# Written-out program, vectors in dense stretches, FFN norm sums about a shift: one step of a hybrid decoder

## The reference

```
x <- LN(alpha*x + 1/2*(1+g1)*SwiGLU_1(mod(x; s1, sc1)))
x <- LN(alpha*x + (1+g2)*W_out[pool_mix(u_A) | gelu(u_G)*RGLRU(conv(u_B))]),  [u_A|u_B|u_G] = mod(x; s2, sc2) @ W_in
x <- LN(alpha*x + 1/2*(1+g3)*SwiGLU_2(mod(x; s3, sc3)))
mod(x) = x*(1+scale(c)) + shift(c);  the nine vectors s1, sc1, g1, ... g3 of a layer come from silu(c) @ W_ada + b_ada
LN: mean, variance, (x-mean)*rstd, times ln_g, plus ln_b
SwiGLU: (silu(h @ w_gate) * (h @ w_up)) @ w_down, 21 tiles of 128 wide
```

## Time and profile before

| what | value |
|---|---|
| time, median of 3 runs | 1088.82 us (1086.84 to 1091.44) |
| span of the profiled execution, its own time | 1091.2 us |
| PE busy | 1016.7 us, 93% of the span |
| DVE busy | 647.9 us, 59% |
| ACT busy | 552.8 us, 51% |
| POOL busy | 104.8 us, 10% |
| moved by transfers | 234.46 MB, 215 GB/s on the mean |

### The profile page before, as it was taken

How to read it: one execution, slowest core, us unless ns; L and a number is a source line. 1 busy time by engine, 2 the same in 40 slices (tenths; PEclk the granted TensorE clock), 3 DMA queues, 4 the chain that set the end, 5 groups by cost and what they waited for, 6 DMA issues and landing times. The chain is left out here.

```text
span 1091.2 us, 25203 instructions
## 1 busy us (share of the span) xinstructions
PE 1016.7 (93%) x9660; PEld 983.8 (90%) x9660; DVE 647.9 (59%) x909; ACT 552.8 (51%) x642; POOL 104.8 (10%) x195
## 2 busy tenths in 40 slices
PE   5799999998997999999969999999799889999996
PEld 3699999987995999999959999999698779999995
DVE  1455554558797754556465545454869885555554
ACT  1556564244664656553237565533539456565432
POOL 8000000005001700000040000000310050000000
PEclk9699999999999999999989999999899999999998
DMA  9898856796679576655678976498747956655621
GB/s 290 264 280 231 227 166 234 232 317 226 224 260 319 142 213 164 187 168 186 204 236 230 258 222 188 152 319 284 255 145 275 315 160 190 188 161 172 194 76 40
DMA packets 279223, 234.46 MB, mean 215 GB/s; under 512 B 7328, under 2 KB 240922, under 8 KB 279123
## 3 DMA queue, kind: packets, MB, share of 16 engines
q1 hardware_dynamic: 277040, 229.70, 68.0%
q0 software_dynamic: 1792, 2.54, 0.9%
q10 hardware_dynamic: 306, 1.12, 0.3%
HBM read 232.06 MB, written 1.78 MB: 214 GB/s over the span
## 5 line engine op out<-in xcount | busy, mean ns | idle before, releaser
L853 DVE TENSOR_TENSOR w_lo<-raw,w_hi 128x2048 fp32r<-128x2048 f32 x156 | 358.3, 2298 | 255.9 <-ACT w_hi L688 255.3
L439 PE MATMUL bank<-m_hi,w_hi 128*128 128x264 f32 x1664 | 479.9, 288 | 18.8 <-DVE m_lo L897 14.8
L440 PE MATMUL bank<-m_lo,w_hi 128*128 128x264 f32 x1664 | 476.6, 286 | 0.0
L441 PE MATMUL bank<-m_hi,w_lo 128*128 128x264 f32 x1664 | 476.0, 286 | 0.0
L688 ACT ACTIVATE w_hi<-raw 128x2048 fp32r<-128x2048 f32 x156 | 298.2, 1911 | 170.3 <-PE bank L441 122.0
L439 PEld LDWEIGHTS bank<-m_hi,w_hi 128*128 128x128 f32 x1664 | 318.3, 191 | 22.0 <-DVE m_lo L897 16.2
L440 PEld LDWEIGHTS bank<-m_lo,w_hi 128*128 128x128 f32 x1664 | 318.4, 191 | 0.1
L441 PEld LDWEIGHTS bank<-m_hi,w_lo 128*128 128x128 f32 x1664 | 316.9, 190 | 0.0
L439 PE MATMUL bank<-h_hi,w_hi 128*128 128x264 f32 x672 | 192.2, 286 | 0.0
L441 PE MATMUL bank<-h_hi,w_lo 128*128 128x264 f32 x672 | 191.1, 284 | 0.0
L440 PE MATMUL bank<-h_lo,w_hi 128*128 128x264 f32 x672 | 191.0, 284 | 0.0
(11 more groups left out here) (180 smaller groups left out, 649.6 us busy)
## 6 DMA issues: line engine op xcount, KB each, us to landing
raw<-in_ffn_wgu_dram SPq DMA_DIRECT2D x168, 512.0 KB, 5.1
ada_raw<-in_w_ada_dram SPq DMA_DIRECT2D x72, 1024.0 KB, 8.9
raw<-in_ffn_wdown_dram SPq DMA_DIRECT2D x48, 512.0 KB, 3.6
raw<-in_ffn_wdown_dram SPq DMA_DIRECT2D x48, 384.0 KB, 4.2
raw<-in_w_in_dram SPq DMA_DIRECT2D x24, 512.0 KB, 10.5
raw<-in_w_out_dram SPq DMA_DIRECT2D x16, 384.0 KB, 3.9
raw<-in_w_out_dram SPq DMA_DIRECT2D x8, 256.0 KB, 3.2
x_rows<-in_x_prompt_dram ACTq DMA_DIRECT2D x1, 1024.0 KB
```

The lines of the kernel that those rows point to most:

```text
L439: pe.matmul(out, hi, r_hi, start=start, stop=False)
L440: pe.matmul(out, hi, r_lo, start=False, stop=False)
L441: mm = pe.matmul(out, lo, r_hi, start=False, stop=stop)
L853: dve.tensor_tensor(w_lo[:, slot], raw[:, slot], w_hi[:, slot].bitcast(F32), ALU.subtract)\
```

## The change

The program is written out: no loop over layers and none over UP units, so each of the 18 vectors and each unit has its own place (a vector's number is 9 times the layer plus its index from s1 = 0 to g3 = 8).

- A table `AFTER` gives the place of each vector on PE: (8, 1) puts the first half of vector 2 behind unit 8, its second half behind unit 9, the transposes behind the next. Nine vectors stand in UP and DOWN stretches (2, 3, 4, 8, 9, 10, 12, 13, 14), three in the gap of an FFN norm (5, 11, 15), 6 and 16 in the mixer, 7 behind unit 43 inside OUT of layer 0, 17 behind the variance of the mixer norm of layer 1, 0 and 1 at the start. `LOAD_BEHIND` puts its load into SP's queue.
- The FFN norm's sums are taken about a shift, the mean of the first four tiles, which DVE subtracts from all eight before the last two are finished. Sums of z and of its square over tiles 0 to 5 go to PE before the last product, and what follows is a mean and a square matmul for each of the tiles 6 and 7. DVE makes the variance as the mean of squares less the square of the mean.
- Normalising is one operation per tile on DVE, z times coefficient times rstd (`full`), ACT adds the shift and rounds to m_hi, and one more on DVE makes m_lo (`low`); the mean is subtracted in pairs of tiles between them.
- The first two units behind a norm are taken together, tile by tile: 12 matmuls for each tile of m_hi and m_lo.
- POOL's `finish_x` begins when the third unit behind the norm is split.
- Units of DOWN and OUT are split over their own width. In OUT the second half goes over tiles 0 and 1, then 2 to 4, then 5 to 7, residuals are added one tile at a time, and the split of the first unit of the next FFN stands between the residuals of tiles 1 and 2.

```diff
+    AFTER = {2: (8, 1), 3: (15, 1), 4: (24, 1), 5: (32, 0), 6: (38, 0), 7: (43, 0), 8: (54, 1), 9: (62, 1),
+             10: (71, 1), 11: (77, 0), 12: (89, 1), 13: (96, 1), 14: (104, 1), 15: (110, 0), 16: (116, 0),
+             17: (122, 0)}
...
+    LOAD_BEHIND = {2: (4, 5)}
+    for a in range(3, VECTORS):
+        first, apart = AFTER[a - 1]
+        LOAD_BEHIND[a] = (first + 6, first + 6 + apart)
...
-                def norm_beside(i, v, after):
-                    ada_part(v, 0)
-                    mean(i)
-                    ada_rest(v)
-                    variance(i)
-                    ada_part(after, 0)
-                    if i == 1:
-                        turn_rows()
-                    ada_part(after, 1)
+            def beside(g):
+                if g in FIRST_HALF:
+                    ada_part(FIRST_HALF[g], 0)
+                if g - 1 in FIRST_HALF:
+                    ada_part(FIRST_HALF[g - 1], 1)
+                if g - 2 in FIRST_HALF:
+                    ada_turns(FIRST_HALF[g - 2])
...
+            def up_phase(l, f, together, vector):
+                g0 = l * UNITS + UP[f]
+                for j in range(together):
+                    ready(pe, g0 + j)
+                for k in range(DT):
+                    pe.wait_ge(m_ready, l * MODS + f * (DT + 2 + DT) + k + 1)
+                    for j in range(together):
+                        product(bank[2 * j][:, 0:T], *weight((g0 + j) % SLOTS, k), m_hi[:, k], m_lo[:, k],
+                                k == 0, k == DT - 1, gate_done)
+                        product(bank[2 * j + 1][:, 0:T], *weight((g0 + j) % SLOTS, DT + k), m_hi[:, k], m_lo[:, k],
+                                k == 0, k == DT - 1, units_done)
...
+                            if pair == 3 and third == 2 and i == 1:
+                                pe.wait_ge(sums_ready, 2 * l + f + 1)
+                                stat(bank[MEAN], mean_w, zsum[:], True, False)
+                                stat(bank[VAR], mean_w, sqs[:, 0], True, False)
...
+                        if pair == 2 and third == 0:
+                            pe.wait_ge(first_sum, 2 * l + f + 1)
+                            stat(bank[MEAN], shift_w, zsum[:], True, True).then_inc(shift_out, 1)
+                        beside(g)
...
+            def ffn_stats(l, f):
+                n, s = l * 3 + 2 * f, l * 14 + f * 9
+                pe.wait_ge(evicted, n * DT + 7)
+                stat(bank[MEAN], mean_w, z[:, 6], False, False)
+                pe.wait_ge(squared, s + 4)
+                stat(bank[VAR], mean_w, sqs[:, 6], False, False)
+                pe.wait_ge(evicted, n * DT + 8)
+                stat(bank[MEAN], mean_w, z[:, 7], False, True).then_inc(mean_out, 1)
+                pe.wait_ge(squared, s + 5)
+                stat(bank[VAR], mean_w, sqs[:, 7], False, True).then_inc(var_out, 1)
...
+                act.wait_ge(rows_out, l + 1)
+                if l:
+                    act.wait_ge(rows_stored, l * 6 * 16)
+                act.activation(s_rows[0:96], bank[ROWS][0:96, :], ACT.Copy).then_inc(rows_ready, 1)
+                if l:
+                    ada_copies(17)
+                act.wait_ge(var_out, l * 3 + 2)
...
-                    own.did(dve.reciprocal(rstd[:], rstd[:]))
-                    own.wait()
-                    for m in range(DT):
-                        o = dve.tensor_tensor(z[:, m, 0:TP], z[:, m, 0:TP], rstd[:, 0:TP], ALU.mult)
+                def full(m):
+                    dve.scalar_tensor_tensor(sq[:, m, 0:TP], z[:, m, 0:TP], coef[:, 0, m, 0:1], rstd[:, 0:TP],
+                                             ALU.mult, ALU.mult).then_inc(scaled, 1)
+                def low(m):
+                    dve.wait_ge(m_hi_done, first + (m + 2 if m else 1))
+                    return dve.scalar_tensor_tensor(m_lo[:, m, 0:TP], sq[:, m, 0:TP], coef[:, 1, m, 0:1],
+                                                    m_hi[:, m, 0:TP].bitcast(F32), ALU.add, ALU.subtract)
...
+                full(1)
+                for m in range(2, DT):
+                    if m in late:
+                        subtract_mean(m)
+                        dve.wait_ge(less_mean, n * DT + m + 2)
+                    full(m)
+                    low(m - 1).then_inc(m_ready, 1)
+                low(DT - 1).then_inc(m_ready, 1)
...
+                    if i == 7:
+                        dve.wait_ge(shift_out, k + 1)
+                        shift = wide(bank[MEAN][:, 0:T], 2)
+                        for a in (0, 2):
+                            dve.tensor_tensor(z[:, a:a + 2], z[:, a:a + 2], shift, ALU.subtract).then_inc(centred, 1)
+                        for a in (4, 6):
+                            own.did(dve.tensor_tensor(z[:, a:a + 2], x[:, a:a + 2], shift, ALU.subtract))
...
+                split(g0 + 4)
+                split(g0 + 5)
+                tiles_done = l * 7 + 1
+                dve.wait_ge(tile_done, tiles_done + 1)
+                residual([(0, 0)], G2, x, evicted)
+                dve.wait_ge(units_done, g0 + 4)
+                residual([(1, 1)], G2, x, evicted)
+                n = l * 3 + 1
+                dve.wait_ge(evicted, n * DT + 2)
+                own.did(dve.tensor_tensor(zsum[:], z[:, 0], z[:, 1], ALU.add))
+                split(g0 + 6)
+                for m in (2, 3, 4, 5, 6, 7):
+                    if m in (4, 7):
+                        dve.wait_ge(units_done, g0 + (5 if m == 4 else 6))
+                    else:
+                        tiles_done += 1
+                        dve.wait_ge(tile_done, tiles_done + 1)
+                    residual([(m, m)], G2, x, evicted)
...
+            def finish_x(l, i):
+                n = l * 3 + i
+                pool.wait_ge(rstd_ready, n + 1)
+                ready(pool, l * UNITS + (IN, UP[1], UNITS)[i] + 2)
+                for m in range(DT):
+                    pool.wait_ge(less_mean, n * DT + m + 1)
+                    pool.tensor_tensor(x[:, m], z[:, m], rstd[:], ALU.mult).then_inc(x_scaled, 1)
+                    pool.wait_ge(x_scaled, n * DT + m + 1)
+                    pool.tensor_scalar(x[:, m], x[:, m], ln_g_of(l, i)[:, m:m + 1], ln_b_of(l, i)[:, m:m + 1],
```

More of the change, by code:

```diff
@@ new lines, in _, with product, weight @@
+            pe.wait_ge(init_read, 1 + DT)
+            def product(out, hi, lo, r_hi, r_lo, start, stop, done=None):
+                pe.matmul(out, hi, r_hi, start=start, stop=False)
+                pe.matmul(out, hi, r_lo, start=False, stop=False)
+                mm = pe.matmul(out, lo, r_hi, start=False, stop=stop)
+                if stop and done is not None:
+                    mm.then_inc(done, 1)
+                return mm
+            def weight(slot, i):
+                return w_hi[:, slot, i * P:(i + 1) * P], w_lo[:, slot, i * P:(i + 1) * P]
@@ L674, in _ @@
+                t.then_inc(fin_out, 1)
         @block.scalar
@@ new lines, in mixer @@
+                if l == 0:
+                    ada_copies(vector + 2)
+                act.activation(spare[:], eps[:], ACT.Sqrt)
+                for a in range(0, DT, 2):
+                    square(sq[:, a:a + 2], z[:, a:a + 2], less_mean, (l * 3 + 1) * DT + a + 2)
+                act.wait_ge(rows_out, l + 1)
[4 more added lines that the diff above has]
+                    ada_copies(17)
@@ new lines, in mixer @@
+                dve.wait_ge(mean_out, n + 1)
+                dve.wait_ge(evicted, (n + 1) * DT)
+                for a in range(0, DT, 2):
+                    dve.tensor_tensor(z[:, a:a + 2], z[:, a:a + 2], wide(bank[MEAN][:, 0:T], 2), ALU.subtract)\
+                       .then_inc(less_mean, 2)
+                if l == 0:
+                    finish_vector(vector + 2)
+                coefficients(l, 2)
+                split(g0 + 7)
+                dve.wait_ge(less_mean, (n + 1) * DT)
+            split(0)
```

1330 lines of the change are left out of this document (728 added, 602 removed).

## The result

The changed kernel took 1072.14 us (median of 4 runs, 1071.33 to 1072.58), the kernel before 1088.26 (4 runs, 1086.84 to 1091.44) on the same chip: ratio 0.986, 95% interval 0.983 to 0.988. On a second chip, beside 13 runs of the kernel before, it was 1072.24 against 1091.58, ratio 0.983 (0.981 to 0.986). So it is faster, by 16 to 19 us, where the forecast of 1056 promised 33. The direction and the range held; the size did not.

A forecast was written before the change was run, and what follows sets the result against it. Dense stretches were taken as bound by PE's own work, with norms and the end between them. Terms summed to −32.5 from a span of 1091.2, giving 1058.7 and, with 2.4 off, 1056 us; range 1036 to 1080.

The forecast's parts named there:

- The FFN norm of 7.1: Last to first product around an FFN norm falls from 19.9 to about 7.1 us; two such norms give −25.6.
- the end of 16.4: The end, without subtract, squares and eight variance matmuls in series, falls from 21.6 to about 16.4 us: −5.2.
- the clock of the first units: First units behind three norms start at clock 1.00 after shorter PE idle, 1.7 us less each: −5.1.
- the price of a dense vector: A vector in dense FFN stretches costs 4.1 us; nine stand there instead of four: +20.5.
- the second FFN of layer 0: Layer 0's FFN 2 and its norm, the stage's terms together: −10.5 us.
- rival B: Partial stalls in dense stretches from GpSimd's x operations meeting DVE, up to 32 us: 1068–1088, at worst 1089; chance 0.15.
- rival C: Vector loads in lumps of 2–4 MB ahead of raw loads starve dense code: 1150 if nothing is absorbed; chance 0.07.
- the mixer norm: DVE's split waits for a raw behind 4 MB of vector; layer 0 gains 0.8, layer 1 loses 2.3: +1.5.
- Moves in the start, waits for splits of pairs and the parameter preparation cancel: These three effects were costed at nothing, taken to cancel within 1.4 us.
- The base: The sum used the profiled span of 1091.2; the shown runs' median, 1088.82, is 2.4 lower, taken off at the end.
- A: The raw is there in time and the mixer norms shrink too: −21, 1035 us; chance 0.20.

The follow-up runs named there:

- e7: The changed kernel without the wait that keeps GpSimd's pass over x behind the third unit's split: 1088.16 us.
- e2: The changed kernel with vector 17's halves read behind the last FFN's first and second units instead of ahead of the first: 1060.09 us.
- e3: The changed kernel with loads of vectors 7 and 17 reading only 64 of 2048 columns of each chunk: 1049.32 us.
- e6: The changed kernel with vector 7 read earlier, vector 17 moved into UP, vector 7's copies ahead of splits, DVE's split between residuals 4 and 5: 1045.70 us.
- e9: The changed kernel with PE multiplying the identity by itself behind OUT in the mixers, 7 and 52 products: 1069.17 us.
- e12: e6 with GpSimd's transfers of layer 1's parameter and state rows and state copies behind the split of unit 1: 1042.92 us.
- e10: e6 with the transfer of x_prompt issued by SP ahead of the first vector chunk instead of by ACT beside it: 1045.66 us.
- e1: The changed kernel with DVE's split of the next FFN's first unit moved behind the mixer norm's subtraction: 1063.72 us.
- e4: The kernel before, unchanged, profiled a second time: span 1091.5 us, time 1093.07 us.
- e5: The changed kernel, unchanged, run again on another chip with a second profile: 1072.24 us.
- e11: The changed kernel with the nine UP and DOWN vectors computed by 32 matmuls instead of 128, the rest left out: 1070.85 us.

## Why the prediction was right, and where it was wrong

**Right, and at the forecast size.** The FFN norm of 7.1 (measured 7.1 three times), the end of 16.4 (16.9), the clock of the first units (forecast −5.1; the first 96 products behind the three norms take 12.3 instead of 13.6, 14.3 and 14.2, together −5.2), the price of a dense vector (4.3 for 4.1), and with it the second FFN of layer 0 (−10.5 forecast, −11.7 measured). The norm's terms up to the reciprocal add up to 4.9, where the prediction writes 5.2; the trace has 5.1, because DVE's subtract for tiles 0 and 1 ends behind the root. For the end's 16.4 no terms are shown. The pass of GpSimd, rival B, leaves no gap above 0.40 us on PE where the change put it; e7 shows that it costs 16 us beside the norm. Lumps of vector loads in dense code, rival C, were absorbed: behind the start PE has no gap above 0.40 in the UP and DOWN stretches.

**The step that failed in size: the mixer norm.** The mechanism was named (the split between the residuals, behind 4 MB), and e2, e3 and e6 show it. The term was priced at +1.5, and the two stages came out 7.9 above their forecast (11.3 by the second profiles). Two parts show in the rows. The raw came 19.9 and 19.6 us behind the issue of the first chunk (311.72 to 331.60, 821.31 to 840.94), where 18.1 was worked out from the earlier trace rows: 1.5 to 1.8 each, and no run shows why. And the chain behind the last residual was priced at full clock: it took 12.8 in layer 0 instead of 10.4, and 16.3 in layer 1 instead of 13.5. Of that e9 gives back 2.0 and 1.5 by keeping PE busy ahead of it. The row of the kernel before that said 0.71 for a statistics matmul stood in a stretch with clock 1.00. In the changed kernel PE had waited 13.2 ahead of these matmuls in layer 1, and 2.7 and 3.2 in layer 0 with only two transposes in between; the clock was 0.54 and 0.50, and such a matmul took 0.9 to 1.25. SP's issue, 0.7 later in the stage than forecast, adds to it, and the residuals took about half a microsecond less. The stage that all this was compared with was a long one, too: in the second profile of the kernel before the two norms take 21.8 and 22.7, where the earlier trace rows has 24.3.

**The step that failed by being left out: the start.** "Moves in the start, waits for splits of pairs and the parameter preparation cancel" was taken without looking at what GpSimd's queue carries there. The start and the first FFN came out 5.0 above forecast, 4.7 of it in three parts. The first product is 1.6 later: e12 shows the rows of layer 1 behind this, and e10 shows that the order of x is not. PE's transposes of layer 1's parameters now stand among layer 0's products, 1.3 from 67.66, where before they stood in the norm between the layers (563.52):

```profile
67.66 0.57 PE L433 MATMUL bank<-ident,st_rows 120*128 120x120 f32 x4
...
68.78 0.25 PE L433 MATMUL bank<-ident,q_rows 36*128 36x36 f32 x1
```

And the first 96 products took 1.8 longer, 1.5 of it in the second unit at clock 0.77. That part is not the change's: the second profile of the kernel before has it too, and e1 does not. What decides it is not shown.

**The base.** Four more microseconds lie between the profiled span, a long execution's, and the median off which the difference was taken (e4, e5). A difference of spans, −20.6, was compared with a difference of medians, −16.1 on one chip and −19.3 on the other.

**What the rivals were worth.** A, the mixer norms shrinking too, needed the raw in time: it is e6, 1045.7, with all the work. A's own 1035 had layer 1's norm at 13.2 (344.1 behind 330.9), short even of the 13.5 (344 to 357.5) that the prediction gives the chain with vector 17 in it; with the raw in time and vector 17 in its place that norm took 18.9 (e3). The prediction did not ask what other order SP's queue could have; the order chosen cost 23 us (e3), more than the whole change gained.

## What to carry to other kernels

A transfer that nobody needs yet, written ahead of one that an in-order engine waits for, can cost its whole landing time (here 4 MB, 11.5 us in e2). Look at what each engine has queued behind the wait: moving one instruction (e1) handed the wait to the next engine, while moving the transfer (e2, e6) removed it. When a loop is written out, loads that were once a layer's own start may all fall into the first microseconds, where everything waits for transfers (e12). Price PE's work behind a long wait from rows at the lower clock (e9). And take the forecast's base from the same execution as its rows, or from several: the kernel before took 1086 to 1097 us from one execution to the next.

## What the runs showed of the hardware

Matmuls that write four different groups of 32 partitions run side by side: 64 of them and 16 of them take the same time, 1.96 and 1.93 us (e11). In the trace of the changed kernel the four of a group start 0.007 apart and the groups 0.11 apart; in e11 the single ones are 0.11 apart. The Trainium skill, "TensorE: Matmul & The Clock Gate", part on packing small matmuls, states that tiles of the array at different positions overlap, started about 4 ns apart; the trace agrees, with 7.

GpSimd and DVE hold up each other's operations. An m_lo of 0.48 that began behind a GpSimd operation took 0.97, and a GpSimd operation of 0.75 that began behind a w_lo took 2.78, beside a w_lo of 2.49 (e7). The Trainium skill, "SBUF — State Buffer", section on who interferes with whom, states that a DVE instruction with two SBUF inputs contends with a GpSimd instruction that reads SBUF, and that the order of issue decides which of the two is blocked; these rows agree.

Small transfers of GpSimd's queue, 496 packets and 0.65 MB more, delayed the two vectors that SP reads at the start (8 MB) by 2.7 us, when the 16 transfer engines were busy nine tenths of most slices (e12).
